# Neighbourhood attention blocks of an encoder kernel: scores of two pairs of heads issued together, and the reciprocals' spreading moved

## The reference, cut to what matters

```python
kg = k[:, :, key_idx, :]          # 8 x 32 keys about each block of 16 columns
vg = v[:, :, key_idx, :]
scores = einsum('bhrcqe,bhrcke->bhrcqk', qg, kg) * hd ** -0.5
scores = scores + bias            # learned, relative position
p, _ = masked_softmax(scores, col_ok)
out = einsum('bhrcqk,bhrcke->bhrcqe', p, vg)
```

## Time and profile before

| | |
|---|---|
| median of three runs | 2966.77 us |
| profiled execution, its own time | 2967.2 us |
| its span, first to last instruction | 2965.4 us |
| mean granted TensorE clock | 0.996 |
| PE busy | 99% of the span |
| PE weight loads busy | 93% |
| DVE, ACT, POOL busy | 68%, 42%, 31% |

### The profile page before, as it was taken

One profiled execution on the slowest core, in us unless ns is written; L12 is line 12 of the kernel. 1 busy time (PEld: TensorE's weight loads), 2 busy tenths in 40 slices (PEclk: granted clock), 3 DMA queues, 4 the chain that ended last, 5 costly groups with the idle time before them and its releaser, 6 DMA issues.

```text
span 2965.4 us, 50329 instructions
## 1 busy us (share of the span) xinstructions
PE 2927.1 (99%) x19328; PEld 2757.3 (93%) x19328; DVE 2025.8 (68%) x3695; ACT 1231.9 (42%) x2377; POOL 931.3 (31%) x762
## 2 busy tenths in 40 slices
PE   9999999999999999999999999999999999999998
PEld 7888887999999999999988888889999999999998
DVE  7977856388744447687879778563986444476786
ACT  5444544454322225444554444444534222255342
POOL 1211212755522226001442111137556222250013
PEclk9999999999999999999999999999999999999998
DMA  4111022333222225734621110223232222258245
GB/s 160 46 59 53 22 91 71 108 115 118 88 78 70 70 70 188 232 121 156 198 93 46 51 59 22 100 78 129 87 116 82 70 70 70 97 165 271 87 144 197
DMA packets 153451, 307.53 MB, mean 104 GB/s; under 512 B 16128, under 2 KB 76160, under 8 KB 152960
## 3 DMA queue, kind: packets, MB, share of 16 engines
q1 hardware_dynamic: 148784, 291.74, 30.0%
q10 hardware_dynamic: 4432, 12.58, 1.1%
HBM read 238.73 MB, written 57.67 MB: 100 GB/s over the span
## 4 chain that ended last, share of the span: by engine, by line
PE 85%; DVE 9%; issue 2%; POOL 2%; ACT 1%; DMA 1%; SPq 0%; ACTq 0%; DVEq 0%; POOLq 0%
PE PS L2847 26%; PE PS L2849 25%; PE PS L2848 25%; PE PS L3013 3%; PE PS L2997 2%; PE PS L2981 1%; PE PS L2969 1%; POOL OSS L1397 1%; DVE PT L2592 1%; PE PS L2885 1%; DVE PR L2545 1%; DVE SW L2459 1%; DVE ACCUM L2166 0%; PE PS L2941 0%; POOL ML L1489 0%
## 5 line engine op out<-in xcount | busy, mean ns | idle before, releaser
L2847 PE MATMUL PS<-XH,WH 128*128 128x512 f32 (+1 forms) x1152 | 432.6, 376 | 8.5 <-DVE VD L2437 2.8
L2849 PE MATMUL PS<-XH,WL 128*128 128x512 f32 (+1 forms) x1152 | 410.3, 356 | 0.0
L2848 PE MATMUL PS<-XL,WH 128*128 128x512 f32 (+1 forms) x1152 | 408.8, 355 | 0.0
L1425 POOL TENSOR_TENSOR GL<-GR,GH 128x512 fp32r<-128x512 f32 x186 | 251.8, 1366 | 366.2 <-ACT GH L1792 304.5
L2847 PE MATMUL PS<-DHH,DWH 128*128 128x384 f32 (+1 forms) x1056 | 328.3, 311 | 0.0
L2849 PE MATMUL PS<-DHH,DWL 128*128 128x384 f32 (+1 forms) x1056 | 326.6, 309 | 0.0
L2848 PE MATMUL PS<-DHL,DWH 128*128 128x384 f32 (+1 forms) x1056 | 325.8, 309 | 0.0
L2847 PEld LDWEIGHTS PS<-XH,WH 128*128 128x128 f32 x1152 | 217.8, 189 | 65.6 <-issue 27.1
L2849 PEld LDWEIGHTS PS<-XH,WL 128*128 128x128 f32 x1152 | 217.8, 189 | 32.6
L2848 PEld LDWEIGHTS PS<-XL,WH 128*128 128x128 f32 x1152 | 218.4, 190 | 24.5
L2848 PE MATMUL PS<-CL0T,GH 128*128 128x384 f32 x704 | 238.4, 339 | 0.0
(11 more groups left out here) (271 smaller groups left out, 8284.8 us busy)
## 6 DMA issues: line engine op xcount, KB each, us to landing
GR<-w_gu SPq DMA_DIRECT2D x62, 768.0 KB, 4.2
RAW<-w_in SPq DMA_DIRECT2D x48, 512.0 KB, 3.6
DHR<-hidden SPq DMA_DIRECT2D x66, 320.0 KB, 4.4
DWR<-w_down SPq DMA_DIRECT2D x66, 256.0 KB, 3.8
S3B<-w_down SPq DMA_DIRECT2D x66, 256.0 KB, 3.3
GR<-w_gu SPq DMA_DIRECT2D x62, 256.0 KB, 2.8
T3B<-hidden SPq DMA_DIRECT2D x44, 320.0 KB, 3.9
hidden<-S1T SPq DMA_DIRECT2D x44, 192.0 KB, 1.9
```

Source lines behind the costliest of these rows:

```text
L1425: nc.gpsimd.tensor_tensor(GL[v % 2][:, m, :, :], GR[v % 2][:, m, :, :], GH[v % 2][:, m, :, :].bitcast(F32), ALU.subtract).then_inc(s_wlo_r ...
L2847: nc.tensor.matmul(out, wh, xh, start=first, stop=False, skip_group_check=reopened)
L2848: nc.tensor.matmul(out, wh, xl, start=False, stop=False, skip_group_check=reopened)
L2849: return nc.tensor.matmul(out, wl, xh, start=False, stop=last, skip_group_check=reopened)
```

## The change

In the neighbourhood blocks alone:

- The scores of pairs 0 and 1 are issued together before the loop, those of pairs 2 and 3 in unit 2, 4 and 5 in unit 6, 6 and 7 in unit 10, 8 and 9 in unit 14. Units 0, 4, 8, 12 and 16 issue none. Odd pairs use banks 1 and 3, even pairs 0 and 2.
- `spread_recip` is issued right behind the turn of the odd unit, one unit later than before, and DVE's `y` behind the low part of that unit instead of ahead of it.

In all blocks `exp(u)` of an even u from 4 on waits in addition until POOL has copied the reciprocals of units u-4 and u-3.

```diff
@@ ACT, exp
                     act.wait_ge(s_masked, first + u + 1)
+                    if u >= 4 and u % 2 == 0:
+                        act.wait_ge(s_recip, NP * nb + u // 2 - 1)
@@ DVE, mask
+                    if b not in DIL:
+                        ps = PS[:, 2 * (u % 2) + u // 2 % 2, :]
@@ DVE, loop
                 for u in range(NU):
-                    if u > 1 and u % 2:
+                    if b in DIL and u > 1 and u % 2:
                         y(u // 2 - 1)
...
+                    if b not in DIL and u > 1 and u % 2:
+                        y(u // 2 - 1)
                     if u + 2 < NU:
                         mask(u + 2)
@@ PE, scores
-                    if pair:
-                        pe.wait_ge(s_masked, first + 2 * pair)
+                    side = pair % 2 if b not in DIL else 0
+                    if pair > side:
+                        pe.wait_ge(s_masked, first + 2 * pair - 2 * side)
...
-                            last = nc.tensor.matmul(PS[:, 2 * h, 0:nkt * P], q[own, i * P:(i + 1) * P], keys,
+                            last = nc.tensor.matmul(PS[:, 2 * h + side, 0:nkt * P], q[own, i * P:(i + 1) * P], keys,
@@ PE, before the loop
                 scores(0)
+                if b not in DIL:
+                    scores(1)
@@ PE, loop
                     turn(u)
-                    if u % 2 == 0 and u + 2 < NU:
+                    if b not in DIL and u > 1 and u % 2:
+                        spread_recip(u // 2 - 1)
+                    if b in DIL and u % 2 == 0 and u + 2 < NU:
                         scores(u // 2 + 1)
+                    if b not in DIL and u % 4 == 2 and u + 2 < NU:
+                        scores(u // 2 + 1)
+                        scores(u // 2 + 2)
                     fill(u)
...
-                    if u and u % 2 == 0:
+                    if b in DIL and u and u % 2 == 0:
                         spread_recip(u // 2 - 1)
```

## The result

The changed kernel takes 2970.43 us (median of 20 runs, 2966.75 to 2974.54), the kernel before 2966.51 us in as many: a ratio of 1.0014, 95% interval 1.0008 to 1.0021, or +2.4 to +6.2 us. The forecast was +5.2 (2972.0), with a range of 2970 to 2974.5. Of all executions behind these and the later figures one, of the experiment `tiles_moved`, took 9906.20 us for a reason that isn't known, and its ratio leaves it out.

What follows compares the result with a forecast made beforehand. PE, busy 99% of the span, bounds the kernel, except that a DVE chain holds even intervals at 2.09 us. 2 x (0.9 + 1.7) = +5.2 us on 2967.2 gives 2972.4, median 2972.0, range 2970 to 2974.5.

Steps and rivals of the forecast that it cites:

- A second pair: In a merged session, three couples at the 0.18 pitch: 0.54 us for a sample pair, 0.36 for a prompt pair.
- The upper bound of 0.64: Cost in us of a second sample pair if a new query tile cost an entry like the first couple's 0.28.
- the floor: Even intervals never under 2.09 us, by `values`, `across`, two additions and low part; removing scores there gives nothing.
- The drain of v: Block 3, unit 16: the fill waits while DVE drains the v group, no longer covered by scores; +0.69 us.
- The wait in unit 4: Block 3: a drain of one instruction takes 1.0 us against 0.96 of cover; +0.1 us (0 to 0.2).
- The spreads: Blocks 3 and 4: +0.11 us in odd units, regained in even ones on PE's path; net +0.11 and +0.54.
- rival B: Moved `y` is late, so `values` of odd pairs and DVE's mask wait; +3 to +7 us, around 2976; chance 0.16.
- Units 9 and 10 of block 4: DVE's tap comes later anyway in unit 9; unit 10's 2.46 us interval hides all but 0.03 of added scores.
- The waits on ACT at nothing: The new wait in `exp`, 80 times at 0 to 0.14 us each, taken as 0 since ACT isn't late.
- The sum: Block 3 +0.9 us and block 4 +1.7 us, doubled for two layers: +5.2 us.
- Rival A: Every merge saves 0.36 us and the spreads cost nothing: 7.2 us gained, 2959.6 us; chance 0.12.
- rival C: Gains and losses cancel, about 2967 us; a moved spread or merged pair costs half of that taken; chance 0.14.

Runs made afterwards that it cites:

- tiles_moved: The changed kernel with the same number of fill tiles put in other units of blocks 3 and 4; 0.9995 of the time of the kernel before.
- add_late: The changed kernel with DVE's low part ahead of the additions in even units of blocks 3 and 4; 1.0025 of the kernel before.
- chosen_merges: Sessions merged only where the emptied unit has a long fill, spreads and `y` where they stood before the change; 0.9988 of the kernel before.
- spread_only: The moved spreads and `y` alone, with one session per pair as in the kernel before; 1.0006 of the kernel before.
- wait_na_only: The changed kernel with ACT's new wait only in blocks 3 and 4, so 48 waits fewer in the dilated blocks; 1.0012 of the kernel before.
- merge_only: The merged sessions alone, with spread and `y` where they stood before the change; 1.0009 of the kernel before.

## Why the prediction was right

Differences between turns' starts, block 3 and block 4 of layer 0, in us:

| from turn, block | before | forecast | after |
|---|---|---|---|
| 0, block 3 | 2.13 | 2.13 | 2.13 |
| 2, block 3 | 2.76 | 3.19 | 3.18 |
| 4, block 3 | 4.12 | 3.2 | 3.07 |
| 12, block 3 | 2.09 | 2.09 | 2.09 |
| 16, block 3 | 3.85 | 3.71 | 3.70 |
| 0, block 4 | 2.64 | 2.13 | 2.13 |
| 4, block 4 | 2.09 | 2.09 | 2.09 |
| 6, block 4 | 2.09 | 2.5 | 2.50 |
| 8, block 4 | 2.36 | 2.09 | 2.35 |
| 9, block 4 | 3.83 | 3.83 | 3.65 |
| 10, block 4 | 2.46 | 2.49 | 2.65 |
| 14, block 4 | 2.09 | 2.13 | 2.13 |
| 16, block 4 | 1.96 | as before | 1.96 |

- A second pair costs the pitch and no entry: right, 0.54. The upper bound of 0.64 wasn't needed.
- Scores taken out of a unit at the floor save nothing: right, and the step that decides. It was read from one unit, in which PE had 1.88 us of work and the next turn came at 2.09; add_late shows that the additions are part of the chain, tiles_moved and chosen_merges that the loss goes away with the short units. That an even interval is never under 2.09 was too strong: unit 16 of block 4 has 1.96 before and after. Nor does unit 8 sit at 2.09, but at 2.36, where a tap stands beside it. Both kept their interval, so the sum didn't suffer.
- The drain of v: right. The fill of unit 16 waited 0.45 us of idle PE (447.92), 0.69 by starts. The wait in unit 4, forecast at 0.1 from a difference of 0.04 (1.0 against 0.96), didn't come.
- The spreads: 0.11 in each odd unit, right.
- `y` late (rival B): did not come in the changed kernel; `values` waited once, 0.14 us, in unit 9 with the tap. Its cover of 0.2 to 0.3 us is real, though (the 2.45 in it adds up to 2.43): with two tiles in an odd unit, in tiles_moved, it was gone, and `values` waited 0.19 us for YB. In add_late it waited 0.46 us in unit 9.
- Units 9 and 10 of block 4: wrong by 0.18 and 0.16 in opposite directions. spread_only, in which `y` moves and no session is merged, has the same 3.64 and 2.65, so it is the moved spreads and `y` that do it; I left `y`'s move out of DVE's order there.
- The waits on ACT at nothing: right for the dilated blocks by wait_na_only; for the others it fits the intervals, and no run tests it alone.
- The sum: 2.4 us a layer against 2.6. Block 3 took 75.04 us where 75.3 was forecast, +0.66 and not +0.9: the drain in unit 4 and rounding. Block 4's +1.7 came as +1.71, in part by luck, since the errors of units 9 and 10 cancel. The median's +3.9 is at the low end of the stated range; 0.4 of the difference is the sum of squares in the one profiled pair, and the rest is within the interval.

Rival A (the gain whole, -7.2) fell by the time itself and by merge_only, rival C by the intervals, which show each cost in its full size.

## What to carry to other kernels

Work on a saturated engine is worth its time only where that engine ends the interval; find, for each interval between two of its waits, the chain that would end it if the engine had nothing to do, and take out work only above that floor, or move other work in. A merge of two stretches is two edits, one that fills a place and one that empties another: price both places. An instruction moved behind another in one engine's order moves everyone who waits for it; the reader of the result that was put last is the next wait.

## What the runs showed of the hardware

- A 64-row session costs 0.36 us to enter and leave between 128-row matmuls (0.90 against 0.54), whether six matmuls stand in it or twelve.
- Stretches near the end run at the lower clock level with PE busy throughout, and not the same ones in every profile: granted clock 0.75 and 0.57 in two neighbouring windows of 5 us in the kernel before, 1.00 and 0.75 in the changed one. Between these two profiles that is 1.6 us, and 3.1 us between before and merge_only (PE 3.7 us late at 2930, 0.6 at 2944.5). That is as much as the change itself, so PE's starts matched ahead of such a stretch are the better measure.
